# Four transformer-like layers in float32 on one core: other accumulator banks, another order of three side chains, narrower waits

## What is computed

```python
h = x @ w_in                    # layer 0: 2048 x 20480
... attention of three dilations, 16 heads; y = o * silu(z)
x = layer_norm(alpha * x + y @ w_out)
h = x @ w_in                    # layer 1: c_q 512, c_kv 512, k_pe 64, z 2048 columns
q = rms_norm(c_q) @ w_uq; kv = rms_norm(c_kv) @ w_ukv; k_pe = rope(k_pe)
... attention of 16 heads; y = o * silu(z); x = layer_norm(alpha * x + y @ w_out)
x = x + even_layer(x)           # layer 2: 8 attention heads, then 4 mLSTM heads
x = x + odd_layer(x)            # layer 3: gated recurrence and gated delta rule
```

## Time and profile before

| what | value |
|---|---|
| median of 3 runs | 2582.0 us (2581.06 to 2582.91) |
| the profiled execution | 2581.53 us, its span 2579.8 us, so 1.7 us lie around the span |
| PE busy | 2485.1 us, 96% of the span |
| DVE, ACT, POOL busy | 55%, 47%, 7% |
| TensorE's mean granted clock | 0.988 of full speed |
| weights moved | 405.63 MB on SP's queue |

### The profile page before, as it was taken

The page is one execution under the profiler, slowest core; times in us unless marked ns, Lnnn a source line. Parts: engine busy times, 40 slices in busy tenths (PEclk is TensorE's granted clock), DMA queues, the critical chain, the costliest instruction groups (busy, mean ns, idle before and its releaser), DMA issues.

```text
span 2579.8 us, 30127 instructions
## 1 busy us (share of the span) xinstructions
PE 2485.1 (96%) x12030; PEld 2065.6 (80%) x12030; DVE 1426.7 (55%) x1881; ACT 1219.4 (47%) x1644; POOL 184.5 (7%) x171
## 2 busy tenths in 40 slices
PE   8999999999999999989999989999999999999889
PEld 6888888888888888867877868888788878888777
DVE  5545464546464555554445565554445566667674
ACT  4444444444444445344555355554444454434453
POOL 1101010101010100000000000000000002122100
PEclk9999999999999999989999989999999999999999
DMA  7545454555555555545433555556555554333334
GB/s 242 185 154 189 162 181 163 163 180 169 173 175 169 163 180 173 194 130 180 146 104 114 191 157 178 178 167 192 154 176 170 176 172 133 104 114 115 98 127 135
DMA packets 350241, 414.50 MB, mean 161 GB/s; under 512 B 19019, under 2 KB 285477, under 8 KB 349589
## 3 DMA queue, kind: packets, MB, share of 16 engines
q1 hardware_dynamic: 348692, 405.63, 49.0%
q0 software_dynamic: 1408, 6.94, 0.7%
HBM read 410.42 MB, written 2.10 MB: 160 GB/s over the span
## 4 chain that ended last, share of the span: by engine, by line
PE 89%; DVE 5%; ACT 3%; issue 2%; POOL 1%; SPq 0%; DMA 0%; ACTq 0%; DVEq 0%
PE ps L541 26%; PE ps L543 25%; PE ps L542 25%; PE ps L581 2%; PE ps L954 2%; PE ps L696 1%; ACT whi L1092 1%; DVE wlo L1621 1%; DVE work L2088 1%; PE ps L683 1%; PE ps L755 1%; PE ps L688 1%; PE ps L754 1%; PE ps L767 0%; PE ps L746 0%
## 5 line engine op out<-in xcount | busy, mean ns | idle before, releaser
L1621 DVE TENSOR_TENSOR wlo<-raw,whi 128x1024 fp32r<-128x1024 f32 (+1 forms) x774 | 953.8, 1238 | 836.5 <-ACT whi L1092 834.0
L541 PE MATMUL ps<-whi,xh 128*128 128x512 f32 (+1 forms) x3072 | 1230.2, 400 | 20.0 <-ACT work L1278 8.2
L543 PE MATMUL ps<-whi,xl 128*128 128x512 f32 (+1 forms) x3072 | 1198.6, 390 | 0.0
L542 PE MATMUL ps<-wlo,xh 128*128 128x512 f32 (+1 forms) x3072 | 1197.1, 390 | 0.0
L1092 ACT CAST whi<-raw 128x1024 fp32r<-128x1024 f32 (+1 forms) x774 | 801.3, 1040 | 817.9 <-PE ps L543 812.8
L541 PEld LDWEIGHTS ps<-whi,xh 128*128 128x128 f32 x3072 | 580.1, 189 | 140.8 <-issue 12.1
L543 PEld LDWEIGHTS ps<-whi,xl 128*128 128x128 f32 x3072 | 578.9, 188 | 121.1
L542 PEld LDWEIGHTS ps<-wlo,xh 128*128 128x128 f32 x3072 | 580.0, 189 | 109.8
L2364 POOL TENSOR_TENSOR work<-work 128x512 f32<-128x512 f32 x48 | 77.1, 1605 | 882.6 <-DVE work L1806 488.6
L1170 ACT ACTIVATE work<-work,small 128x128 f32<-128x128 f32 (+1 forms) x80 | 46.1, 577 | 165.1 <-DVE small L1731 165.1
L954 PEld LDWEIGHTS ps<-work 128*128 128x128 f32 x544 | 68.2, 193 | 16.7 <-issue 7.0
(11 more groups left out here) (371 smaller groups left out, 1393.0 us busy)
## 6 DMA issues: line engine op xcount, KB each, us to landing
raw<-in_dsa_w_in SPq DMA_DIRECT2D x320, 512.0 KB, 4.5
raw<-in_ev_w_in SPq DMA_DIRECT2D x144, 512.0 KB, 4.5
raw<-in_od_w_in SPq DMA_DIRECT2D x96, 512.0 KB, 4.4
raw<-in_mla_w_in SPq DMA_DIRECT2D x48, 512.0 KB, 4.5
raw<-in_dsa_w_out SPq DMA_DIRECT2D x32, 512.0 KB, 4.6
raw<-in_mla_w_out SPq DMA_DIRECT2D x32, 512.0 KB, 4.7
raw<-in_ev_w_out SPq DMA_DIRECT2D x32, 512.0 KB, 4.5
raw<-in_od_w_out SPq DMA_DIRECT2D x32, 512.0 KB, 4.8
```

What stands on the lines that cost most here:

```text
L541: pe.matmul(o, xh[:, k, tokens[tb]], hi, start=start and s + l == 0, stop=False)
L542: pe.matmul(o, xh[:, k, tokens[tb]], lo, start=False, stop=False)
L543: m = pe.matmul(o, xl[:, k, tokens[tb]], hi, start=False, stop=stop and s + l == 2)
L1621: dve.tensor_tensor(whole_half(wlo[:, h % 4], n), whole_half(raw[:, h // 2 % 4, 2 * (h % 2):2 * (h % 2) + 2], n), whole_half(whi[:, h % 4] ...
```

## The change: what it does

- Layer 0: slab s of pair p takes bank `2 * ((5 * p + s) % 2)`, so all 40 slabs alternate. PE's slab waits for the eviction of the slab two before. `out_bank` no longer depends on the layer, and `y_place` turns y of layer 0 in banks 0 and 1 at first.
- Layer 1, first slabs: the k_pe columns go to bank 4, the c_kv slab to banks 2 and 3. The gate slabs wait for `out0`, `out2` and ACT's `tanh` of the slab two before, not for DVE's gate.
- Layer 1, `norms`: the copy and the rotation of k_pe come first, squares and norms after them and one to a tick; PE's second turning of k_pe comes at tick 9, not 4.
- Layer 1, first quad: its q unit waits for `tanh` of gate slab 2 and the turned c_q, its k and v unit for those of slab 3 and c_kv.
- Layer 1, `attention1`: PE's first two jobs and DVE's rotation wait for `out2` alone, the third job for `out3`. ACT copies v behind the first two jobs' copies.
- Layer 2: `attention2` has one more empty tick ahead of its heads on all three engines. `mlstm` on PE waits for `q` instead of `o`, and has three ticks instead of one between its turnings and L880; ACT and DVE likewise.

```diff
         la_a = marks("la_a", "out0 rows out2 kp sq*4 kpt")
         la_d = marks("la_d", "t k ms norm")
...
+        def out_bank(s):
+            return 2 * (s % 2)
+        def bank0(pair, s):
+            return 2 * ((5 * pair + s) % 2)
...
                     if s >= 2:
                         pe.wait_ge(*e0_a.at(pair, f"out{s - 2}"))
                     elif pair:
-                        pe.wait_ge(*e0_a.at(pair - 1, ("out4", "out3")[s]))
-                    project(side, N, 2 * (s % 2), 0 if pair + s == 0 else None,
+                        pe.wait_ge(*e0_a.at(pair - 1, f"out{3 + s}"))
+                    project(side, N, bank0(pair, s), 0 if pair + s == 0 else None,
...
-                yield from turns(3)
+                yield from turns(8)
                 pe.wait_ge(*la_d.at(0, "k"))
...
-                pe.wait_ge(*e1_a.all(quad + 1))
+                pe.wait_ge(*e1_a.at(quad, "out2"))
...
                 for n, (src, c, m, hh0) in enumerate(jobs):
+                    if n == 2:
+                        pe.wait_ge(*e1_a.at(quad, "out3"))
...
             project(nothing, 512, 0, 1)
-            few_columns(nothing, 64, 2)
-            pe.wait_ge(*la_a.at(0, "out0"))
-            project(nothing, 512, 0)
+            few_columns(nothing, 64, Q)
+            project(nothing, 512, 2)
...
-            pe.wait_ge(*la_a.at(0, "out2"))
             for slab in range(4):
-                if slab >= 2:
-                    pe.wait_ge(*g1_d.at(slab - 2, "gate"))
+                pe.wait_ge(*(g1_a.at(slab - 2, "tanh") if slab >= 2 else la_a.at(0, f"out{2 * slab}")))
...
-            pe.wait_ge(*g1_d.at(3, "gate"))
-            pe.wait_ge(*ct_d.at(3, "lo"))
...
                         if p or quad:
                             pe.wait_ge(*e1_a.at(quad - 1 + p, f"out{2 * (1 - p) + kind}"))
+                        else:
+                            pe.wait_ge(*g1_a.at(2 + kind, "tanh"))
+                            pe.wait_ge(*ct_d.at(1 + 2 * kind, "lo"))
...
             def mlstm(head):
-                pe.wait_ge(*e4_a.at(head, "o"))
+                pe.wait_ge(*e4_a.at(head, "q"))
...
-                yield
+                yield from turns(3)
                 pe.wait_ge(*p4_a.at(head, "copy1"))
                 pe.wait_ge(*p4_d.at(head, "sel"))
...
             def norms():
+                act.wait_ge(*la_p.at(0, "kraw"))
+                act.copy(L1.kp, ps[:, Q + 3, 0:P].rearrange("p (t c) -> p t c", t=TB)).then_inc(*la_a.up("kp"))
+                yield
                 act.wait_ge(*la_a.at(0, "out2"))
...
+                        yield
-                act.wait_ge(*la_p.at(0, "kraw"))
-                act.copy(L1.kp, ps[:, Q + 3, 0:P].rearrange("p (t c) -> p t c", t=TB)).then_inc(*la_a.up("kp"))
...
                 h0 = 16 + 4 * quad
-                act.wait_ge(*hd_p.at(h0 - 1, "pv"))
-                act.wait_ge(*e1_a.all(quad + 1))
-                act.copy(L1.v, L1.kv[:, :, :, P:]).then_inc(*p1_a.up("v"))
                 yield
...
+                    if n == 1:
+                        act.wait_ge(*hd_p.at(h0 - 1, "pv"))
+                        act.wait_ge(*e1_a.all(quad + 1))
+                        act.copy(L1.v, L1.kv[:, :, :, P:]).then_inc(*p1_a.up("v"))
...
                 dve.tensor_tensor(L1.t2[:, :, 0, 32:64], L1.kp[:, :, 0:32], sinb[:, :, 32:64], ALU.mult).then_inc(*la_d.up("t"))
+                yield from turns(2)
                 dve.wait_ge(*la_d.at(0, "t"))
                 dve.tensor_tensor(L1.kp, L1.t1[:, :, 0], L1.t2[:, :, 0], ALU.add).then_inc(*la_d.up("k"))
-                yield
+                yield from turns(4)
+                dve.wait_ge(*la_a.at(0, "sq3"))
+                dve.tensor_scalar(small[:, 4:8], small[:, 0:4], 1.0 / L1.R, EPS, ALU.mult, ALU.add).then_inc(*la_d.up("ms"))
+                yield from turns(2)
+                dve.wait_ge(*la_g.at(0, "pow"))
...
-                dve.wait_ge(*e1_a.all(quad + 1))
+                dve.wait_ge(*e1_a.at(quad, "out2"))
...
                 dve.tensor_tensor(xv, xv, bc(small[:, 56:64], 2, P), ALU.mult).then_inc(*p2_d.up("norm"))
-                yield from turns(4)
-                yield
+                yield from turns(6)
...
                                          op0=ALU.add, op1=ALU.mult).then_inc(*p4_d.up("gate"))
-                yield
+                yield from turns(3)
```

More of the change, by code:

```diff
@@ L236, in build_program @@
         m1_g = marks("m1_g", "zero low high")
-        la_a = marks("la_a", "out0 rows out2 sq*4 kp kpt")
-        la_d = marks("la_d", "ms norm t k")
+        la_a = marks("la_a", "out0 rows out2 kp sq*4 kpt")
+        la_d = marks("la_d", "t k ms norm")
         la_g, la_p = marks("la_g", "pow"), marks("la_p", "kraw k")
@@ L242, in build_program @@
         e1_a = marks("e1_a", "out*4")
-        p1_a, p1_d, p1_p = marks("p1_a", "v copy*6"), marks("p1_d", "t r"), marks("p1_p", "turn*6")
+        p1_a, p1_d, p1_p = marks("p1_a", "copy0 copy1 v copy2 copy3 copy4 copy5"), marks("p1_d", "t r"), marks("p1_p", "turn*6")
         c2_d = marks("c2_d", "gq copy bias0 bias1")
@@ L462, in y_place @@
                 return place, 7 if i < 4 else 2 + i % 2
-            return place, 2 + i % 2 if layer == 0 or i >= EARLY[layer] else i % 2
-        def out_bank(layer, s):
-            return 2 * ((s + (layer == 0)) % 2)
+            return place, 2 + i % 2 if i >= EARLY[layer] else i % 2
+        def out_bank(s):
+            return 2 * (s % 2)
+        def bank0(pair, s):
+            return 2 * ((5 * pair + s) % 2)
         def weights():
@@ L626, in last_product @@
                         pe.wait_ge(*free[s])
-                    unit(side, 4 * QUARTERS[layer][m], N, out_bank(layer, s), m == 0, m == 3, fine, {0: more, 4: late}.get(u))
+                    unit(side, 4 * QUARTERS[layer][m], N, out_bank(s), m == 0, m == 3, fine, {0: more, 4: late}.get(u))
                 for s in range(2):
                     pe.wait_ge(*add_d.at(layer, f"add{s}"))
-                    project(nothing, N, out_bank(layer, s), fine=fine)
+                    project(nothing, N, out_bank(s), fine=fine)
             def attend(h, scores, turned, pv, gap, last):
@@ L1269, in scalar @@
                         act.wait_ge(*p0_p.at(pair - 1, ("turn1", "turn2", "turn3", "turn5", "turn5")[s]))
-                    b = 2 * (s % 2)
+                    b = bank0(pair, s)
                     if s < 4:
@@ L1276, in scalar @@
                             act.wait_ge(*p0_d.at(pair - 1, "z"))
-                        act.copy(L0.h[:, 8], ps[:, 0:2, 0:HALF])
-                        act.activation(L0.h[:, 9], ps[:, 0:2, HALF:N], ACT.Copy, scale=0.5).then_inc(*e0_a.up("out4"))
+                        act.copy(L0.h[:, 8], ps[:, b:b + 2, 0:HALF])
+                        act.activation(L0.h[:, 9], ps[:, b:b + 2, HALF:N], ACT.Copy, scale=0.5).then_inc(*e0_a.up("out4"))
                 run(side)
@@ L1320, in scalar @@
             act.wait_ge(half_done, half[0])
-            act.copy(L1.kpt[0:64], ps[0:64, 2, 0:S]).then_inc(*la_a.up("rows"))
+            act.copy(L1.kpt[0:64], ps[0:64, Q, 0:S]).then_inc(*la_a.up("rows"))
             project(nothing)
             act.wait_ge(half_done, half[0])
-            act.copy(L1.cc[:, 1], ps[:, 0:2, :]).then_inc(*la_a.up("out2"))
+            act.copy(L1.cc[:, 1], ps[:, 2:4, :]).then_inc(*la_a.up("out2"))
             side = norms()
@@ L1684, in add @@
                 def add(q):
-                    b = out_bank(layer, q)
+                    b = out_bank(q)
                     c = slice(q * N, (q + 1) * N)
@@ L1851, in norms @@
             def norms():
-                dve.wait_ge(*la_a.at(0, "sq3"))
-                dve.tensor_scalar(small[:, 4:8], small[:, 0:4], 1.0 / L1.R, EPS, ALU.mult, ALU.add).then_inc(*la_d.up("ms"))
-                yield
-                dve.wait_ge(*la_g.at(0, "pow"))
-                for i in range(4):
-                    m = dve.tensor_scalar(L1.cc[:, i // 2, i % 2], L1.cc[:, i // 2, i % 2], small[:, 4 + i:5 + i], None, ALU.mult)
-                m.then_inc(*la_d.up("norm"))
                 yield
@@ L1863, in norms @@
                 dve.tensor_tensor(L1.t2[:, :, 0, 32:64], L1.kp[:, :, 0:32], sinb[:, :, 32:64], ALU.mult).then_inc(*la_d.up("t"))
+                yield from turns(2)
                 dve.wait_ge(*la_d.at(0, "t"))
                 dve.tensor_tensor(L1.kp, L1.t1[:, :, 0], L1.t2[:, :, 0], ALU.add).then_inc(*la_d.up("k"))
-                yield
+                yield from turns(4)
[3 more added lines that the diff above has]
+                dve.wait_ge(*la_g.at(0, "pow"))
+                for i in range(4):
+                    m = dve.tensor_scalar(L1.cc[:, i // 2, i % 2], L1.cc[:, i // 2, i % 2], small[:, 4 + i:5 + i], None, ALU.mult)
+                    if i % 2 == 0:
+                        yield
+                m.then_inc(*la_d.up("norm"))
                 yield
```

1 line of the change is left out of this document (removed).

## The result

| | kernel before | changed kernel |
|---|---|---|
| median, us | 2582.45 (2581.06 to 2585.11, 4 runs) | 2554.44 (2553.80 to 2555.52, 4 runs) |
| the profiled execution, us | 2581.53, span 2579.8 | 2554.72, span 2553.0 |

The ratio is 0.9891, with a 95% interval of 0.9874 to 0.9908: 28.0 us less by the medians, 26.8 by the profiled executions.

A forecast was written before the change was run, and what follows sets the result against it. PE, busy 96% of the span, was taken to bound the kernel, so only its pauses could be won. Terms 10.1 + 1.4 + 2.3 + 3.4 + 1.6 + 2.3 + 0.9 + 2.9 gave 24.9, called 25 us: 2557.0, range 2552 to 2563.

The forecast's parts named there:

- `mlstm`: Layer 2's mLSTM heads: earlier turnings and less wait for `sel`, 0.73 us a head, four times, 2.9 us.
- Layer 0's banks: Layer 0's seven pair boundaries: PE's wait for the pair's last eviction goes, 1.44 us each, 10.1 us.
- c_kv in other banks: Layer 1's first gate slab goes to banks emptied long ago, so its wait goes, 1.4 us.
- `norms`: Layer 1: PE's wait for DVE's rotation of k_pe behind the norms goes, 2.3 us.
- Its low clock: Behind the pause before layer 1's first quad: the 3.40 us at granted clock 0.50 goes too, 1.6 us.
- The doubt raised with layer 3's row: Layer 3's clock falls with shorter pauses, so a some-3-us limit is not borne out; otherwise caused, the sum is 23.4.
- The quads' joints: Layer 1, three joints: the 1.25 us eviction wait goes, 0.5 is given back, 2.3 us in all.
- the second rule: Low-clock work behind a pause varies between runs, acting at layer norm restarts; some 2 us to either side.
- The small waits that change their name: Quads and mLSTM heads: waits stay behind ACT's chain and DVE's `sel`; 20 us less, 2562; chance 0.13.
- The clock in layer 3: Layer 3: more or fewer low stretches, 1.7 us each; 2560.4 or 2553.6; chance 0.13, evenly.
- Layer 0 not about banks: Layer 0's pair starts: something else than the eviction held PE, the 10.1 us stays; 2567; chance 0.03.
- Late weights: Weight transfers over the kernel come late with fewer pauses; at 0.1 us a unit 2595.7; chance 0.01.

The follow-up runs named there:

- l0_only: The kernel before with only layer 0's alternating banks; 2572.22 us against 2583.14, ratio 0.9955.
- norms_back: The changed kernel with layer 1's old order of norms on all three engines, squares and scaling ahead of the key's rotation; 2563.41 us.
- q_gate: The changed kernel with PE again waiting for DVE's gate of the last gate slab before the first quad; 2557.83 us, profiled again 2560.49.
- v_first: The changed kernel with ACT's copy of v ahead of its first two job copies in a quad, as before; 2554.84 us.
- v_last: The changed kernel with ACT's copy of v behind all six job copies, PE's first product with v waiting for it; 2555.67 us.
- sel_first: The changed kernel with DVE's small copy `sel` at the first tick, ahead of the gate, instead of the fourth; 2554.05 us.
- q_tanh: The changed kernel with PE waiting only for ACT's tanh of the last gate slab before the first quad; 2555.02 us.

## Why the prediction was right, point by point

The forecast was 25 us less and 2557.0 in a range of 2552 to 2563; measured were 28.0 and 2554.4. The mechanism was right: the pauses that were named are gone, and most places gave what they were costed at. Some of the closeness is luck: two slips in the working pull in opposite directions and about cancel (0.4 us too little for the joints, 0.3 too much for `mlstm`), the clock behind the first quad's pause was taken for certain and is not, and 0.9 us came where no edit is.

- **Layer 0's banks**, 10.1 us forecast: 10.3 at the boundaries (10.0 by the stage, whose start was 0.3 us longer at the low clock), and l0_only has it alone. Shown. The cover for the split was there: the list of PE's waits has DVE's remainder three times with 7.4 us in all, as before, so none of it at a pair's start.
- **c_kv in other banks** (1.4) and **`norms`** (2.3): 1.39 and 2.31 at their places. The stage of the c_kv slab shows 1.1 only, since the low clock behind layer norm 0 reached 0.5 us further into it. The sum is right, but costing each by itself was not: norms_back shows that without the new order the bank edit's gain would have come back as a longer wait, 3.50 us for 2.14. I had not asked of this pause what was late next.
- **The first quad**: 3.4 forecast, 3.45 measured, and the same in q_gate. **Its low clock**, 1.6: the two profiles differ by that much, but I took it for certain, and q_gate shows it is not. The doubt raised with layer 3's row was right: by the length of the pause alone one cannot tell.
- **The quads' joints**: 2.3 forecast, 2.85 measured (0.94, 0.95 and 0.95). The mechanism was right, ACT's copies behind v and cast; v_first and v_last move it both ways. The size was off: I put 0.5 us of new wait at each joint, and it is 0.35, 0.23 and 0.24. Most of the difference is a slip: PE at 1286.54 and four turnings of 0.13 us give 1287.06, not 1286.95, so the working's own numbers leave 0.25 us of wait for the bank, 0.35 with the scores, and 2.7 us for the three. PE's list shows even less than that, one wait of 0.2 us where I had named 0.4 as the sign; the rest is seen only from start to start. Another reason may be in ACT's rows: v's copy had to wait for the eviction it reads and began 1.09 us behind that eviction's start, while the job's copy begins 0.91 us behind (1264.00 to 1264.91), and all that follows is 0.2 us earlier.
- **`attention2`**: 0.9 and 0.8. **`mlstm`**: 2.9 and 3.5, 0.88 a head for 0.73. I expected 0.4 us of wait for `sel`; sel_first shows that it was 0.24. By the working's own numbers it would have been 0.5 (1811.7 less 1811.2), and the term 2.6. The chain was costed by full durations, and on ACT and DVE the next instruction starts before the one ahead is through. The changed kernel's timeline of ACT and DVE has two copies of 1.11 us in all with the cast 0.97 behind their start, and a remainder of 1.23 us with `sel` 1.14 behind:

```profile
1784.61 1.11 ACT L1417 ACTIVATE work<-ps 128x512 f32<-128x512 f32 x2
1785.58 1.08 ACT L1097 CAST whi<-raw 128x1024 fp32r<-128x1024 f32 x1
1786.69 1.23 DVE L1630 TENSOR_TENSOR wlo<-raw,whi 128x1024 fp32r<-128x1024 f32 x1 [0.61 <-ACT whi L1097]
1787.83 0.21 DVE L2026 COPY work<-work 4x128 f32<-4x128 f32 x1
```

- **Not in the sum**: 0.9 us behind layer norm 1. No slab matmul ahead of the layer norm moved, and the whole difference comes at the first one behind it. It goes with the clock. Counted from the start of layer 1's last slab matmul, the low stretch ended at 22.0 us in the kernel before and at 20.2 in the changed one, and layer 2's first slab matmul came at 26.7 and 25.8. Windows of the same 2 us, from 20.0 to 22.0 us, in the kernel before and in the changed one; PE got through 11 matmuls in the first and 19 in the second:

```profile
1516.90:1518.90 2.00, 2.00 (x11) 1.33 (x10) 2.00 (x6) 1.98 (x5) 0.33 (x2) 0.50 1.01 370
```

```profile
1495.30:1497.30 2.00, 2.00 (x19) 1.53 (x18) 2.00 (x6) 2.00 (x5) 0.25 (x1) 0.96 1.01 396
```

  In the 14 profiles the end of the low stretch goes from 20.0 to 22.8 us and this stage from 129.60 to 131.06 us with it, by about half. It was in the range only, by the second rule. The Trainium skill (TensorE: Matmul & The Clock Gate, Part 1, the clock gate) states that rule for a kernel's start; that it holds behind a pause too is what these profiles show.
- The 28.0 us of the medians against 26.8 of the profiles: the profile of the kernel before is 0.9 us under its median and the changed kernel's 0.3 above. The kernel before had a second low stretch (1.65 us) in its second profile, which the one I worked from lacked. That this is the whole difference is not shown.
- **Rivals.** The small waits that change their name: real in kind, 0.9 us in size, not 5.2. The clock in layer 3: nothing between the two kernels, but in others the stage goes from 511.84 to 514.71 us. The time at the low level is 17.1 us here, 13.7 in v_first and sel_first (512.07 and 512.18 us) and 20.5 in four others, yet the shortest, q_tanh, has 17.1 too: one of its low stretches falls at 2450.4 us, where PE's matmuls lose 0.25 us and have it back one half later, and not at 2236.2, where the changed kernel's costs some 1.6. So where a low stretch falls counts as much as how many there are. Layer 0 not about banks: out. Late weights: PE's list has no wait that ends with a weight's transfer, ACT waits for one twice, 3.1 us in all, as before, and the median is below the forecast: out.
- **The range.** The lower bounds summed to 18 us, which is 2564 and lies outside the range given; the range should have gone to 2564.

## What to carry to other kernels

Pauses of the engine that bounds the kernel can be costed one by one from start to start, and here the sum held to a tenth (25 for 26.8 by the profiles), as long as for each the next thing in the way is found; two pauses that hang on one chain count together, and the shorter edit may be worth nothing alone. When a program differs by a microsecond or two, compare stages between the same instructions of two traces, not the totals: the totals of the kernel before went from 2580.82 to 2585.11 us, stages without a change of clock repeated within 0.1. On an engine whose instructions are issued in a fixed order, the copy that somebody waits for goes ahead of the one that nobody needs yet.

## What was not expected of the hardware

The same program with the same pause of 3.29 us had TensorE at 1.2 GHz for 3.4 us behind it in one execution and at 2.4 GHz in another; over all profiles it fell in 4 of 5. Behind 1.10 and 2.14 us, 8 us apart, it fell in 2 of 3, and without a pause there in none of 8 and none of 10. Behind layer norm 1 the way back to 2.4 GHz came 1.6 us later in one execution of q_gate than in the other, and within 2.8 us over all 14 profiles. So removing a pause of PE gives back its length for certain and some 1.7 us more by chance, and a time near the end of a gain of 1% should be read with both in mind.
